# Attention scores merged in PSUM and divided on eviction, and spatial mixing with high and low weights as one moving operand

## What is computed

```python
def sgu_mixer(h, w_in, ln_g, ln_b, w_s, b_s, w_out):
    z = jax.nn.gelu(h @ w_in)
    u, v = jnp.split(z, 2, axis=-1)
    v = layer_norm(v, ln_g, ln_b)
    ...
    w = jnp.where(causal[None], w_s, 0.0)
    mixed = jnp.einsum('gts,bnsgc->bntgc', w, vp) + b_s.T[:, :, None]
    return (u * mixed) @ w_out, v

def sink_attention(q, k, v, q_pos, k_pos, sinks):
    logits = jnp.einsum('bnqkgd,bnskd->bnkgqs', q, k) * scale
    rel = q_pos[:, :, None] - k_pos[:, None, :]
    valid = (rel >= 0) & (rel < WINDOW) & (k_pos[:, None, :] >= 0)
    logits = jnp.where(valid[None, :, None, None], logits, -jnp.inf)
    m = jnp.maximum(jnp.max(logits, axis=-1, keepdims=True), sink)
    p = jnp.exp(logits - m)
    denom = jnp.sum(p, axis=-1, keepdims=True) + jnp.exp(sink - m)
    return jnp.einsum('bnkgqs,bnskd->bnqkgd', p / denom, v)
```

## Time and profile before

| | |
|---|---|
| median of three runs | 2825.28 us (2822.32 to 2827.12) |
| profiled execution, its own time | 2819.29 us |
| its span | 2817.0 us |
| TensorE busy | 2694.1 us, 96% |
| VectorE busy | 1544.8 us, 55% |
| ScalarE busy | 769.1 us, 27% |
| chain that ended last, by engine | PE 90%, DVE 4%, ACT 3% |
| mean granted clock of TensorE | 0.985 |

### The profile page before, as it was taken

One profiled execution on the slowest core, in us unless ns is written; L12 is line 12 of the kernel. 1 busy time (PEld: TensorE's weight loads), 2 busy tenths in 40 slices (PEclk: granted clock), 3 DMA queues, 4 the chain that ended last, 5 costly groups with the idle time before them and its releaser, 6 DMA issues.

```text
span 2817.0 us, 44039 instructions
## 1 busy us (share of the span) xinstructions
PE 2694.1 (96%) x17722; PEld 2643.8 (94%) x17722; DVE 1544.8 (55%) x2409; ACT 769.1 (27%) x1201; POOL 82.2 (3%) x64
## 2 busy tenths in 40 slices
PE   6999999999899999999998997789999999999998
PEld 5999999999899999999998995479899999999998
DVE  3224667301555555666665768823465555655556
ACT  4233222311322222222223336612322222222221
POOL 0000000001000000000004000001100000000000
PEclk9999999999999999999999999979999999999999
DMA  3111111122111111111111120011111111111112
GB/s 119 38 39 50 48 49 53 54 62 61 31 46 46 46 46 46 46 46 46 46 39 43 45 74 5 1 31 30 38 47 46 46 46 46 46 46 46 46 46 72
DMA packets 191971, 130.55 MB, mean 46 GB/s; under 512 B 6052, under 2 KB 178940, under 8 KB 191868
## 3 DMA queue, kind: packets, MB, share of 16 engines
q1 hardware_dynamic: 181032, 123.74, 14.6%
q10 hardware_dynamic: 10868, 5.79, 0.7%
HBM read 123.32 MB, written 8.15 MB: 47 GB/s over the span
## 4 chain that ended last, share of the span: by engine, by line
PE 90%; DVE 4%; ACT 3%; issue 1%; DMA 0%; SPq 0%; POOL 0%; DVEq 0%; ACTq 0%; POOLq 0%
PE ps L327 70%; PE ps L1676 13%; PE ps L318 2%; PE ps L1708 2%; ACT pr L490 1%; PE ps L867 1%; DVE stt L640 1%; DVE hl L1430 1%; ACT sm L481 1%; DVE sm L636 1%; PE ps L1729 1%; PE ps L884 0%; PE ps L1638 0%; DMA vecs<-in_ffn_conv_b 0%; DVE x L1529 0%
## 5 line engine op out<-in xcount | busy, mean ns | idle before, releaser
L327 PE MATMUL ps<-hh,wh 128*128 128x384 f32 (+1 forms) x2616 | 854.0, 326 | 3.7 <-ACT rbc L1202 2.8
L327 PE MATMUL ps<-hh,wl 128*128 128x384 f32 (+1 forms) x2616 | 853.1, 326 | 0.0
L327 PE MATMUL ps<-hl,wh 128*128 128x384 f32 (+1 forms) x2616 | 852.5, 326 | 0.0
L297 ACT ACTIVATE wh<-wraw 128x1024 fp32r<-128x1024 f32 x200 | 212.5, 1062 | 1160.6 <-PE ps L327 1007.9
L327 PEld LDWEIGHTS ps<-hh,wh 128*128 128x128 f32 x2616 | 491.1, 188 | 4.9 <-ACT rbc L1202 3.8
L327 PEld LDWEIGHTS ps<-hl,wh 128*128 128x128 f32 x2616 | 491.0, 188 | 0.0
L327 PEld LDWEIGHTS ps<-hh,wl 128*128 128x128 f32 x2616 | 491.0, 188 | 0.0
L301 DVE TENSOR_TENSOR wl<-wraw,wh 128x1024 fp32r<-128x1024 f32 x200 | 246.8, 1235 | 361.9 <-ACT wh L297 358.2
L1455 DVE TENSOR_TENSOR a_sb<-ps,rbc 128x768 f32<-128x768 f32 x88 | 84.3, 959 | 465.4 <-PE ps L327 464.7
L327 PE MATMUL ps<-fh,wh 128*128 128x384 f32 (+1 forms) x1008 | 330.2, 328 | 5.3 <-DVE wl L301 5.3
L327 PE MATMUL ps<-fh,wl 128*128 128x384 f32 (+1 forms) x1008 | 330.6, 328 | 0.0
(11 more groups left out here) (234 smaller groups left out, 3165.7 us busy)
## 6 DMA issues: line engine op xcount, KB each, us to landing
wraw<-in_ffn_w_up SPq DMA_DIRECT2D x88, 512.0 KB, 3.9
wraw<-in_ffn_w_down SPq DMA_DIRECT2D x44, 512.0 KB, 3.3
wraw<-in_sgu_w_in SPq DMA_DIRECT2D x32, 512.0 KB, 4.5
wraw<-in_sgu_w_out SPq DMA_DIRECT2D x16, 512.0 KB, 4.1
wraw<-in_attn_w_qkv SPq DMA_DIRECT2D x12, 512.0 KB, 3.5
xin<-in_x_prompt SPq DMA_DIRECT2D x4, 1024.0 KB, 8.1
xm<-in_x_prompt SPq DMA_DIRECT2D x8, 512.0 KB, 3.7
wraw<-in_attn_w_o SPq DMA_DIRECT2D x8, 512.0 KB, 3.9
```

Source lines behind the costliest of these rows:

```text
L297: act.activation(wh[:, s, :], wraw[:, s, :], ACT.Copy).then_inc(w_hi, 1)
L327: ins = pe.matmul(ps[:, BANK[area] + c, 0:cn], w[:, s, col:col + 128], mov[part][:, k, c0:c0 + cn], start=start and i == 0 and n == 0, sto ...
```

## The change

It has two parts. **Mixing:** high and low spatial weights lie side by side (`wt`, `ws`), so `vnh` meets both in one matmul of 256 columns and `vnl` the high ones in one of 128; the two halves of the result lie in five banks (3 to 7) and VectorE adds bias and halves in two passes.

**Attention:** VectorE merges the scores in PSUM itself, the exponentials read PSUM and leave undivided probabilities. ScalarE copies the transposed probabilities to `pt`, VectorE masks one product, `pc`. The output is pt by the v of the block before plus pc by `vd`, the difference between the v of the two blocks, with probabilities as weights and v moving; it lies by token, is evicted by VectorE for two groups at a time (`take_o`) and multiplied there by 1/denominator. Scores run two groups ahead, outputs one behind. `kT` has three buffers, the first three pieces have a bank each, block 0 makes no scores for a block before. Since the outputs lie by token, 64 transposes (`turn_back`) bring them back before the output projection. The lists of ScalarE and VectorE are unrolled.

```diff
...
+            def exps(c):
+                z = c % 2
+                act.wait_ge(s_nm, c + 1)
                 if c >= 2:
...
+                    act.wait_ge(p_t, c - 1)
+                for e in range(2):
+                    for j in range(2):
+                        h = 4 * z + 2 * j + e
+                        ins = act.activation(pr[:, z, 128 * (2 * j + e):128 * (2 * j + e) + 128],
+                                             ps[:, S_BANK[z][e], 256 + 128 * j:384 + 128 * j], ACT.Exp,
+                                             bias=snm[:, c // 2 % 2, h:h + 1], scale=HD ** -0.5,
+                                             accum_out=den[:, c // 2 % 4, h:h + 1])
+                ins.then_inc(p_exp, 1)
...
+            def take_probs(c):
+                act.wait_ge(p_t, c + 1)
                 if c >= 2:
...
+            lo(dve, 0, P_QKV + 6)
+            for m in range(4):
+                t = max(2 * m, 1)
+                dve.wait_ge(tm_free, 65 + m + 1)
+                dve.tensor_tensor(vd[:, t - 1:2 * m + 1, :], qkv[:, t:2 * m + 2, 1280:1536], qkv[:, t - 1:2 * m + 1, 1280:1536],
+                                  sub).then_inc(v_diff, 1)
+            lo(dve, 1, P_QKV + 6)
+            def merge(c):
+                n, g, z = c // 4, c % 4, c % 2
                 b = S_BANK[z][0]
...
+                old = ps[:, b:b + 2, 256:512].rearrange("p e (j n) -> p e j n", j=2)
+                cur = ps[:, b:b + 2, 0:256].rearrange("p e (j n) -> p e j n", j=2)
+                def each(col):
+                    return tb2[:, col:col + 128].unsqueeze(1).unsqueeze(1).to_broadcast([128, 2, 2, 128])
+                dve.wait_ge(s_full, c + 1)
+                if n == 0:
+                    dve.tensor_tensor(old, cur, each(C_NEG), add).then_inc(s_mrg, 1)
+                else:
+                    dve.copy_predicated(old, each(C_CUR).bitcast(i32), cur).then_inc(s_mrg, 1)
+                dve.wait_ge(s_mrg, 2 * c + 1)
+                mx = smx[:, z, :].rearrange("p (e j) -> p e j", e=2)
+                dve.reduce_max(mx, old, AX.X).then_inc(s_mrg, 1)
+                dve.wait_ge(s_mrg, 2 * c + 2)
+                dve.scalar_tensor_tensor(snm[:, c // 2 % 2, 4 * z:4 * z + 4].rearrange("p (j e) -> p e j", e=2), mx, -HD ** -0.5,
+                                         nsk[:, 4 * g:4 * g + 4].rearrange("p (j e) -> p e j", e=2), mult, ALU.min).then_inc(s_nm, 1)
+            def sinks(p):
+                dve.wait_ge(s_nm, 2 * p + 2)
+                dve.tensor_tensor(ssk[:, p % 2, :], snm[:, p % 2, :], nsk[:, 8 * (p % 2):8 * (p % 2) + 8], sub).then_inc(s_sink, 1)
+            def denominators(p):
+                dve.wait_ge(p_exp, 2 * p + 2)
+                dve.wait_ge(p_sink, p + 1)
+                dve.tensor_tensor(den[:, p % 4, :], den[:, p % 4, :], ssk[:, p % 2, :], add).then_inc(dn_ok, 1)
+                dve.wait_ge(dn_ok, 2 * p + 1)
+                dve.reciprocal(den[:, p % 4, :], den[:, p % 4, :]).then_inc(dn_ok, 1)
+            def mask(c):
                 z = c % 2
...
+                dve.wait_ge(p_cp, c + 1)
+                if c >= 6:
+                    dve.wait_ge(o_full, c - 1)
+                dve.tensor_tensor(pc[:, z, :].rearrange("p (h n) -> p h n", h=4), pt[:, z, :].rearrange("p (h n) -> p h n", h=4),
+                                  tb2[:, C_CURT:C_CURT + 128].unsqueeze(1).to_broadcast([128, 4, 128]), mult).then_inc(p_msk, 1)
+            def take_o(p):
+                dve.wait_ge(dn_ok, 2 * p + 2)
+                dve.wait_ge(o_full, 2 * p + 2)
+                dve.tensor_tensor(qkv[:, p // 2, 512 * (p % 2):512 * (p % 2) + 512].rearrange("p (h d) -> p h d", d=HD),
+                                  ps[:, 1 + p % 2, :].rearrange("p (h d) -> p h d", d=HD),
+                                  den[:, p % 4, :].unsqueeze(2).to_broadcast([128, 8, HD]), mult).then_inc(o_ok, 1)
             dve.wait_ge(nsk_ok, 1)
             merge(0)
             merge(1)
-            normalise(0)
-            merge(2)
-            for_steps(dve, step)
-            dve.wait_ge(zero_a, 4)
+            sinks(0)
+            for c in range(GROUPS_A):
+                if c + 2 < GROUPS_A:
+                    merge(c + 2)
+                if c % 2 and c + 2 < GROUPS_A:
+                    sinks(c // 2 + 1)
+                if c >= 4:
+                    mask(c)
+                if c % 2 and c > 1:
+                    take_o(c // 2 - 1)
+                if c % 2:
+                    denominators(c // 2)
+            take_o(PAIRS_A - 1)
...
                 if c >= 2:
-                    pe.wait_ge(s_mrg, 2 * (c - 2) + 1)
-                for old in range(2):
+                    pe.wait_ge(p_exp, c - 1)
+                for old in range(2 if n else 1):
                     for j in range(2):
                         for e in range(2):
                             ins = pe.matmul(ps[:, S_BANK[c % 2][e], 256 * old + 128 * j:256 * old + 128 * j + 128],
                                             qT[64 * e:64 * e + 64, 2 * g + j, :],
-                                            kT[64 * e:64 * e + 64, (n + old) % 2, (g - e) % NKV, :], start=True, stop=True)
+                                            kT[64 * e:64 * e + 64, (n - old) % 3, (g - e) % NKV, :], start=True, stop=True)
                 ins.then_inc(s_full, 1)
...
             def output(c):
                 n, g = c // 4, c % 4
...
+                pe.wait_ge(p_cp, c + 1)
+                if n:
+                    pe.wait_ge(p_msk, c - 3)
+                    pe.wait_ge(v_diff, 4)
+                if c >= 4 and c % 2 == 0:
+                    pe.wait_ge(o_ok, c // 2 - 1)
+                for h in range(4):
+                    o = ps[:, 1 + c // 2 % 2, 256 * (c % 2) + HD * h:256 * (c % 2) + HD * h + HD]
+                    ins = pe.matmul(o, pt[:, c % 2, 128 * h:128 * h + 128], qkv[:, max(n - 1, 0), 1280 + HD * g:1280 + HD * g + HD],
+                                    start=True, stop=n == 0, skip_group_check=True)
+                    if n:
+                        ins = pe.matmul(o, pc[:, c % 2, 128 * h:128 * h + 128], vd[:, n - 1, HD * g:HD * g + HD],
+                                        start=False, stop=True, skip_group_check=True)
                 ins.then_inc(o_full, 1)
...
+            def turn_back(k):
+                if k >= 2:
+                    pe.wait_ge(h_lo, 24 + k - 1)
+                for n in range(8):
+                    ins = pe.transpose(turned_banks(k)[:, n // 4, 128 * (n % 4):128 * (n % 4) + 128],
+                                       qkv[:, n, 128 * k:128 * k + 128], idn[:, :])
+                ins.then_inc(o_t, 1)
             def wo_tile(m, i=None):
                 area = m % 2
                 pe.wait_ge(free[area], at((A_WO, B_WO)[area] + m // 2, 1, i))
                 pe.wait_ge(w_lo, at(2 * P_WO + m + 1, 2, i))
                 if m == 0:
+                    turn_back(0)
                     for k in range(KT):
+                        if k + 1 < KT:
+                            turn_back(k + 1)
                         pe.wait_ge(h_lo, 24 + k + 1)
...
+                tok = out[:, 0:SEQ].rearrange("p (c n) -> p c n", n=128)
+                smp = out[:, SEQ:T].rearrange("p (b n) -> p b n", n=NT)
+                halves = ps[:, 3:7, :].rearrange("p b (h a n) -> p (b h) a n", a=2, n=128)
+                dve.tensor_tensor(tok, halves[:, :, 0], g.unsqueeze(1).to_broadcast([128, 8, 128]), add)
+                dve.tensor_tensor(smp, ps[:, 7, 0:64].rearrange("p (b n) -> p b n", n=NT),
+                                  g[:, 0:NT].unsqueeze(1).to_broadcast([128, NB, NT]), add).then_inc(biased, 1)
+                dve.wait_ge(biased, at(n + 1, 2, i))
+                dve.tensor_tensor(tok, tok, halves[:, :, 1], add)
+                dve.tensor_tensor(smp, smp, ps[:, 7, 64:128].rearrange("p (b n) -> p b n", n=NT), add).then_inc(free[1], 1)
...
-                        src = (wth, wtl) if t < 8 else (wsh, wsl)
-                        o = ps[:, 3 + t // 3, (t % 3) * 128:(t % 3) * 128 + n]
-                        for r, (a, w) in enumerate(((vnh, src[0]), (vnh, src[1]), (vnl, src[0]))):
-                            ins = pe.matmul(o, a[:, t, :], w[:, gi, :].rearrange("p o n -> p (o n)"),
-                                            start=r == 0, stop=r == 2)
+                        src = wt if t < 8 else ws
+                        bank, col = 3 + t // 2, (t % 2) * 256
+                        pe.matmul(ps[:, bank, col:col + 2 * n], vnh[:, t, :],
+                                  src[:, gi, :, :].rearrange("p o a n -> p (o a n)"), start=t % 2 == 0, stop=False,
+                                  skip_group_check=True)
+                        ins = pe.matmul(ps[:, bank, col:col + n], vnl[:, t, :],
+                                        src[:, gi, 0, :].rearrange("p o n -> p (o n)"), start=False, stop=True,
+                                        skip_group_check=True)
                     ins.then_inc(mixed, 1)
...
```

241 lines of the change are left out of this document (77 added, 164 removed).

## The result

| | before | after |
|---|---|---|
| median of four runs of each | 2824.14 us | 2793.39 us (2791.36 to 2796.61) |
| ratio, with its 95% interval | | 0.989 (0.987 to 0.991) |
| profiled execution, own time / span | 2819.29 / 2817.0 us | 2794.57 / 2792.4 us |
| TensorE busy | 2694.1 us | 2704.7 us |
| VectorE, ScalarE busy | 1544.8, 769.1 us | 1525.5, 750.8 us |

What follows compares the result with a forecast made beforehand. TensorE was taken to bound the mixing, a ScalarE-VectorE ring the prompt's attention. 2819.29 - 11.8 (mixing) - 27 (attention) + 8 (turning back) = 2788.5, plus 6 for the median: 2794.5, written 2795; range 2780 to 2813.

Steps and rivals of the forecast that it cites:

- Mixing: Mixing units: matmuls shrink from 2.93 to 2.05 us in fifteen units, the last unit's tail costs +1.3; sum -11.8 us.
- Its cover: Mixing: VectorE's chain grows to 13.73 us against a period of 13.97, hidden with 0.24 us to spare.
- The rival of 2802: Mixing: VectorE becomes the bound if each new add costs 0.2 more; 0.5 us per unit, +7 us; chance 0.06.
- The ring as the bound of the loop: Prompt's attention before: ScalarE's score copy, VectorE's merge and maximum, ScalarE's exponentials set 4.39 us from group to group.
- TensorE's 3.82 a group: Attention loop after: transposes 0.59, scores 1.09, output 1.71, pieces 0.43 us make TensorE the bound.
- The disputed term: Attention loop: output as 16 entries at 0.107, 1.71 us, set by the weights; upper bound 1.90, lower 1.09.
- the cheap output: Attention loop rival: output takes 1.09 us or less, loop 3.2 to 3.3 us a group, total 2780; chance 0.04.
- The first exponentials: Start of attention: 2.4 us earlier, bringing the first transposes of probabilities to 1695.1.
- Groups 0 to 4 ... 3.0 us each: Loop's start: the first groups have half the output matmuls and are held by hand-overs, ending at 1710.1.
- Turning back: Before the output projection: eight blocks of eight transposes cost +8 us, bounds +6 and +21.
- The rival of a clock that stays at half: Turning back: TensorE stays at half clock throughout, +21 us instead of +8, total 2808; chance 0.12.
- The price of a lost clock: Attention loop rival: a group at half clock takes 6.5 us, 2.7 more; all groups +79, 2874; chance 0.04.

Runs made afterwards that it cites:

- e8: Kernel after with the first of gating's adds over 1024 columns made twice; 2804.45 us.
- e7: Kernel before with the merging in PSUM alone: no ScalarE copy of old scores, one merge pass, exponentials read PSUM; 2807.41 us.
- e6: Kernel after with ScalarE's copy of the scores of the block before put back for groups 4 to 31; 2823.99 us.
- e4: Kernel after with output matmuls 16 columns wide instead of 64, the rest of the output left out; 2820.17 us.
- e11: Kernel after with output matmuls 32 columns wide instead of 64, the rest of the output left out; 2801.53 us.
- e2: Kernel after with the mixing of the kernel before, so the attention part alone; 2803.66 us, ratio 0.993 to the kernel before.
- e9: Kernel after with idle transposes filling two TensorE waits: 30 before the first transposes of probabilities, 64 in the samples' attention; 2783.77 us, ratio 0.985 to before.
- e12: Kernel before with 64 idle transposes in TensorE's wait between the samples' two halves of transposes; 2819.37 us, ratio 0.9986.
- e1: Kernel before with the mixing part of the change alone; 2810.19 us, ratio 0.995 to the kernel before.
- e3: Kernel after without the 64 transposes that bring the outputs back, so the projection gets the wrong layout; 2786.34 us.

## Why the prediction was right, and where it was not

**Mixing: right.** 27 matmuls were to go from 2.93 to 2.05 us and the unit to 13.97; it is 14.02 and the blocks 2.0 to 2.1. Fifteen times 0.83 less the tail is 11.1 us, and the stage lost 11.3, where I had 11.8. The tail, `gating` 1.33 longer, is 1.32.

**Its cover: slightly too large, and its price twice too high.** I had 0.24 us to spare, the trace has 0.14 to 0.21 with the hand-over in it. The rival of 2802 stayed away because the adds took what I had worked out (2.77 us for 2.78). Had they not, e8 shows that a unit pays only half of what VectorE is late, so the 7 us of this rival were too much.

**The ring as the bound of the loop: half of it.** e7 shows that without the copy, and with one pass of the merge less, VectorE stops the loop at 3.95, just 0.44 under the 4.39 of before. e6 shows that a copy costs a group 0.7 us in the new order, but in a ring through TensorE that the kernel before did not have. I read the chain, which hops between ScalarE and VectorE, and not the windows, where VectorE stood at 31.50 of 35.12 us. The forecast didn't suffer, since the change relieves both.

**TensorE's 3.82 a group: right.** 3.89 measured, which is 1.5 us over the 24 full groups. The disputed term, 16 output entries at 0.107 or 1.71 us, takes 1.83 from its first entry to the next instruction (0.112 an entry, 0.16 the first), the transposes 0.54 instead of 0.59. e4 and e11 confirm its reason. The bounds of 1.09 and 1.90 held it; of the cheap output nothing is left.

**The first exponentials: a little better than predicted.** From 1699.36 to the predicted 1695.1 are 4.3 us; the stage up to the first transposes of probabilities lost 5.25.

**"Groups 0 to 4 ... 3.0 us each": the step that failed.** They took 18.2 us instead of 15.0. I had seen the half clock after the wait in the samples' stage and not asked what the wait for the first exponentials would do. With e2's clock they take 15.65. With the clock kept up (e9) the same five groups take 1700.84 - 1686.29 = 14.55 us, so hand-overs were priced rightly and the clock was left out. In all the loop brought 23.4 us in the trace after and 25.9 in e2's; I had kept 27.

**Turning back: +8, measured +8.9 and +7.1.** Right in size and in its parts: 0.87 to 0.89 per block at full clock. The rival of a clock that stays at half is refuted by these rows. I had written that no row tested transposes between matmuls, but the eight in 0.87 us of the earlier trace rows were such a row, and a row against the rival. The Trainium skill, TensorE: Matmul & The Clock Gate, section Part 4: PE-mode transpose, has the rule that the full clock doesn't engage for transposes; e9 disagrees, with 64 of them in a row in 7.21 us at a granted 1.00 and a clock that fell in the same wait without them.

**The price of a lost clock: too low.** I had 6.5 us for a group at half clock; in e4 such groups took 7.3. The kernel after met it in its first groups only.

**The sum.** -11.3 - 23.4 + 8.9 = -25.8 in the profiled executions, -11.3 - 25.9 + 7.1 = -30.1 with e2's clock, -30.75 by the medians, -30.8 predicted. The prediction is right in its parts, with small misses (loop 1 to 4 us too good, mixing 0.5, turning back up to 0.9) inside what the clock's timing moves from run to run. That the medians meet the sum to 0.1 us is luck: my sum was built on stages, and by the stages of the profiled executions it is 5 us too high. The rest of the span is 1.4 us longer in all kernels with turning, and also in e12 (897.13), which has none. This is the clock too: ahead of the last output tile TensorE waits 2.67 us in every trace, and in those with the longer rest, and only in those, the granted clock is then at half for a few us (2751.4 to 2754.8 in after, 2775.2 to 2778.6 in e12; none in before, e1, e3 and e7). Why it falls in some executions and not in others stays open.

## What to carry to other kernels

Before naming a ring as the bound, look at the windows of each engine over some periods: an engine that is 90% busy there is the next bound, whatever the chain says, and it tells what half of the change would bring. When a change makes TensorE the bound of a stretch, ask what its clock will be, and read the granted clock of the stretches like it: here it was at half behind waits of some us, and in stretches of matmuls that moved 16 or 32 columns. Filling a wait of TensorE beside a slow stretch was worth 10 us here, and 16 with work that had to be done anyway; in the kernel before it was worth 3 to 4. And before calling the difference between an added cost and the measured one cover, look at two periods: half of it may have gone to the neighbour, as in e8.

## What the runs showed of the hardware

- An fp32 entry with weights of 128 x 128 takes 0.111 or 0.112 us in the loop whether 16, 32 or 64 columns move (the first behind other matmuls 0.13 to 0.16); with weights of 128 x 64 and 16 columns moving, as in the samples' outputs of e9 at full clock, sixteen take 0.90, 0.056 each.
- TensorE can be busy without a gap and yet fall to half clock: for some 31 us in e4's loop (1719 to 1750), and at 1857 in e9. In e9 64 transposes in a row ran at a granted 1.00, 0.110 us each.
- How long the half clock lasts after a wait differs between executions of the same instructions: until about 4 or 10 us after the first transposes of probabilities, worth 2.5 us of the loop.
- An add over 1024 columns from PSUM takes VectorE 1.14 us from start to start, be the other operand the broadcast bias (351.70 to 352.84) or data from SBUF (353.09 to 354.23).
